# Sums of MLP weight blocks: from on-chip slots to a DRAM buffer, with plain loads into ten slots in turn

## The reference, cut to what matters

```
h = rms_norm(x);  z = h @ w_in                       # 1024 x 10240, split into ten parts
m = gated sum of three branches of z, each @ w_branch[i];  m = m @ w_out
x = x + rms_norm(m)
h = rms_norm(x)
f = square(relu(h @ w_ff1)) @ w_ff2                  # 1024 x 4096, 4096 x 1024
x = x + rms_norm(f)
```

## Time and profile before

| what | value |
|---|---|
| median of three runs | 962.34 us (958.67 to 963.13) |
| the profiled execution | 959.98 us, its span 958.2 us |
| PE busy | 948.2 us, 99% |
| DVE busy | 731.4 us, 76% |
| ACT busy | 430.6 us, 45% |
| POOL busy | 104.4 us, 11% |
| bytes moved | 142.84 MB, mean 149 GB/s |
| plain queue of SP (q1) | 111.32 MB, 32.7% of 16 engines' span |
| POOL's queue (q0), nearly all accumulating transfers | 27.27 MB, 15.4% |

### The profile page before, as it was taken

How to read it: one execution, slowest core, us unless ns; L and a number is a source line. 1 busy time by engine, 2 the same in 40 slices (tenths; PEclk the granted TensorE clock), 3 DMA queues, 4 the chain that set the end, 5 groups by cost and what they waited for, 6 DMA issues and landing times.

```text
span 958.2 us, 13425 instructions
## 1 busy us (share of the span) xinstructions
PE 948.2 (99%) x4838; PEld 809.0 (84%) x4838; DVE 731.4 (76%) x854; ACT 430.6 (45%) x534; POOL 104.4 (11%) x128
## 2 busy tenths in 40 slices
PE   9999999999999999999999999999999999999997
PEld 7888888888888888888888888899889889979985
DVE  4679888888888988886584434599976886796698
ACT  7632333333333322224274323467745745754674
POOL 1100001001100011113100000131101102011110
PEclk9999999999999999999999999999999999999998
DMA  8333223322222122223225333477989679678864
GB/s 325 110 111 105 99 93 96 108 93 93 93 95 102 66 100 96 89 89 132 88 93 215 109 109 110 176 198 192 269 265 245 162 212 246 172 185 260 246 188 132
DMA packets 40731, 142.84 MB, mean 149 GB/s; under 512 B 4720, under 2 KB 4848, under 8 KB 40688
## 3 DMA queue, kind: packets, MB, share of 16 engines
q1 hardware_dynamic: 31728, 111.32, 32.7%
q0 software_dynamic: 7712, 27.27, 15.4%
q10 hardware_dynamic: 1248, 3.67, 1.1%
HBM read 138.05 MB, written 4.19 MB: 148 GB/s over the span
## 4 chain that ended last, share of the span: by engine, by line
PE 82%; DMA 7%; DVE 6%; ACT 3%; issue 2%; SPq 0%; POOL 0%; DVEq 0%; ACTq 0%
PE ps L1590 25%; PE ps L1592 24%; PE ps L1594 24%; DMA glu<-units_in 5%; DVE w_lo L1066 3%; PE ps L1775 2%; PE ps L1779 2%; PE ps L1777 2%; DMA raw_d<-units_in 1%; ACT w_hi L683 1%; PE ps L1716 1%; DVE h_lo L1066 1%; PE ps L1670 1%; ACT h L960 1%; DVE h L1408 1%
## 5 line engine op out<-in xcount | busy, mean ns | idle before, releaser
L1590 PE MATMUL ps<-a_hi,w_hi 128*128 128x512 f32 x576 | 225.7, 392 | 0.0
L1066 DVE TENSOR_TENSOR w_lo<-raw,w_hi 128x1024 fp32r<-128x1024 f32 (+1 forms) x125 | 153.3, 1229 | 94.1 <-ACT w_hi L683 93.4
L1592 PE MATMUL ps<-a_lo,w_hi 128*128 128x512 f32 x576 | 224.2, 389 | 0.0
L1594 PE MATMUL ps<-a_hi,w_lo 128*128 128x512 f32 x576 | 224.1, 389 | 0.0
L683 ACT ACTIVATE w_hi<-raw 128x1024 fp32r<-128x1024 f32 (+1 forms) x125 | 130.2, 1048 | 186.1 <-PE ps L1594 112.9
L1149 DVE SCALAR_TENSOR_TENSOR conf<-glu,cols,conf (+1 forms) x240 | 186.8, 778 | 27.5 <-DVE conf L1149 26.4
L1590 PEld LDWEIGHTS ps<-a_hi,w_hi 128*128 128x128 f32 x576 | 108.1, 188 | 22.7 <-issue 0.5
L1592 PEld LDWEIGHTS ps<-a_lo,w_hi 128*128 128x128 f32 x576 | 108.1, 188 | 22.6 <-issue 0.5
L1594 PEld LDWEIGHTS ps<-a_hi,w_lo 128*128 128x128 f32 x576 | 108.2, 188 | 22.5
L1066 DVE TENSOR_TENSOR w_lo<-glu,w_hi 128x1024 fp32r<-128x1024 f32 x56 | 67.7, 1221 | 37.0 <-ACT w_hi L683 36.9
L1590 PE MATMUL ps<-w_hi,h_hi 128*128 128x512 f32 x224 | 87.9, 393 | 0.4
(11 more groups left out here) (177 smaller groups left out, 1608.7 us busy)
## 6 DMA issues: line engine op xcount, KB each, us to landing
raw<-units_in SPq DMA_DIRECT2D x141, 512.0 KB, 3.2
glu<-units_in SPq DMA_DIRECT2D x26, 512.0 KB, 6.5
glu<-units_in POOLq DMA_DIRECT2D x26, 512.0 KB, 8.3
raw_d<-units_in POOLq DMA_DIRECT2D x24, 512.0 KB, 6.5
raw_v<-units_in SPq DMA_DIRECT2D x16, 512.0 KB, 5.9
raw_d<-units_in SPq DMA_DIRECT2D x8, 512.0 KB, 6.2
conf<-x_in SPq DMA_DIRECT2D x4, 512.0 KB, 6.0
conf<-x_in ACTq DMA_DIRECT2D x1, 2048.0 KB, 8.0
```

The lines of the kernel that those rows point to most:

```text
L1066: return nc.vector.tensor_tensor(dst, src, hi, ALU.subtract)
L1590: nc.tensor.matmul(ps[:, bank, :], left_hi, right_hi, start=first, stop=False, skip_group_check=on_top)
L1592: nc.tensor.matmul(ps[:, bank, :], left_hi, right_lo, start=False, stop=False, skip_group_check=on_top)
L1594: return nc.tensor.matmul(ps[:, bank, :], left_lo, right_hi, start=False, stop=final, skip_group_check=on_top)
```

## The change

The sums of weight blocks are no longer made in the slots. A DRAM buffer `weight_sums` holds, for each of the eight matrices (four quarters, up and down), the four sums of two units each: 64 units of 512 KB.

- In each mixing tile ACT issues four copies of 1 MB, DRAM to DRAM, one for each sum of one matrix: its first block (`copy_first`). Before its third and later tiles it waits until the copies of two tiles before are done.
- POOL adds the second block of product 5's sum, one accumulating transfer of 1 MB per mixing tile, when that tile's copies are done, and the second block of product 7's sum, one per pair of the first gate stage (`two_blocks`). In the second gate stage it adds product 5's sum onto product 6's (`three_blocks`), in the third product 6's onto product 4's (`four_blocks`), one per pair, each behind a wait for the pair before. These transfers are written with a longest piece of 8192 bytes.
- In the MLP each unit is loaded by SP with one plain transfer of 512 KB, from the weights or from the sums, into slot (u - U_FF) mod 10, when the unit ten before it is split. SP waits for all sums ahead of the fifth load.
- `add_block`, `side_load`, `sum_beside`, `slot_of` and the waits that went with them are gone, on SP, POOL, ACT and DVE. PE's program is the same.

The core of the diff:

```
 # SP
-            def ff_load(q, f, product, halves=(0, 1)):
-                    if earlier_in_slot(u) and slot < RAW:
-                        sp.wait_ge(summed, sums_beside(q, f, h) - 2)
-                    elif earlier_in_slot(u):
-                        sp.wait_ge(w_lo_ready, earlier_in_slot(u)[-1] + 1)
+            def ff_load(u):
+                if u - U_FF >= SLOTS:
+                    sp.wait_ge(w_lo_ready, u - SLOTS + 1)
...
+                if product in PLAIN:
+                    src = units_d[U_FF + (2 * q + f) * BLOCK_UNITS + block_at(f, PLAIN[product]) + h]
+                else:
+                    src = sums_d[(2 * q + f) * BLOCK_UNITS + sum_at(product) + h]
+                sp.dma_start(slots[slot], src).then_inc(raw_loaded[slot], 16)
+            for n in range(4):
+                ff_load(U_FF + n)
+            for f in range(2):
+                sp.wait_ge(two_summed[f], 16 * QUARTERS)
+                sp.wait_ge(side_summed[f], 16 * QUARTERS)
+                sp.wait_ge(three_summed[f], 16 * QUARTERS)
+                sp.wait_ge(four_summed[f], 16 * QUARTERS)
...
 # POOL
+            def two_blocks(m, product, summed):
+                q, f = divmod(m, 2)
+                copies = len(SUMS) * (q + 1 if product == 5 else QUARTERS)
+                pool.wait_ge(first_copied[f], 16 * copies)
+                at = U_FF + m * BLOCK_UNITS + block_at(f, SECOND_BLOCK[product])
+                pool.dma_start(sum_of(m, product), units_d[at:at + 2].rearrange("h p n -> (h p) n"),
+                               accum_op=ALU.add, max_dma_last_dim=SUM_BYTES).then_inc(summed[f], 16)
+            def three_blocks(m):
+                f = m % 2
+                pool.wait_ge(two_summed[f], 16 * QUARTERS)
+                pool.dma_start(sum_of(m, 6), sum_of(m, 5), accum_op=ALU.add,
+                               max_dma_last_dim=SUM_BYTES).then_inc(three_summed[f], 16)
...
                 mask_spatial(j % 2, 32 * (j // 2 + 1))
+                if j:
+                    two_blocks(j - 1, 5, two_summed)
+            two_blocks(MATRICES - 1, 5, two_summed)
             for j in range(KT):
+                two_blocks(j, 7, side_summed)
                 pool.wait_ge(conf_tap, KT * (N_OWN + N_NEXT) + N_LATE * (j + 1))
...
+            for m in range(4, MATRICES):
+                behind_pair(KT + m)
+                three_blocks(m)
+            for m in range(MATRICES):
+                behind_pair(2 * KT + m)
+                four_blocks(m)
 # ACT
+            def copy_first(j, f, product):
+                source = j.times(BLOCK_UNITS, U_FF + block_at(f, FIRST_BLOCK[product]))
+                into = j.times(BLOCK_UNITS, sum_at(product))
+                act.dma_start(sums_d[bass.ds(into, 2)].rearrange("h p n -> (h p) n"),
+                              units_d[bass.ds(source, 2)].rearrange("h p n -> (h p) n")
+                              ).then_inc(first_copied[f], 16)
             def mix_tile(u, j, b):
+                if j.first >= 2:
+                    act.wait_ge(first_copied[b], Count(j.first // 2, j.i, 1).times(16 * len(SUMS)))
+                copy_first(j, b, 5)
                 after(u)
...
                 split_hi(u.plus(RING))
+                copy_first(j, b, 7)
...
                 split_hi(u.plus(3 + RING))
+                copy_first(j, b, 6)
...
                 split_hi(u.plus(4 + RING))
+                copy_first(j, b, 4)
```

More of the change, by code:

```diff
@@ L86 @@
 H_SLOT = {"22": 4, "22-21": 0, "11-21": 0, "11": 1, "21-22-11": 1, "12": 2, "21+12-11-22": 3}
-LOADED = {1: (0, 0), 2: (1, 0), 3: (1, 1), 5: (0, 0)}
-ADDED = {5: (0, 1), 6: (1, 1), 4: (1, 0), 7: (0, 1)}
+PLAIN = {1: (0, 0), 2: (1, 0), 3: (1, 1)}
+SUMS = (5, 7, 6, 4)
+FIRST_BLOCK = {5: (0, 0), 7: (1, 1), 6: (1, 1), 4: (1, 0)}
+SECOND_BLOCK = {5: (0, 1), 7: (0, 1)}
+SUM_ON_TOP = {6: 5, 4: 6}
+MATRICES = 2 * QUARTERS
 SLOTS = 10
-def slot_of(f, product):
-    return {1: 0, 2: 2, 3: 6, 7: 6}.get(product, 8 if f == DOWN else 4)
+SUM_BYTES = 8192
 def ff_unit(q, f, product, h):
@@ L105, in piece_of, with block_at, sum_at @@
     return q, f, ORDER[f][n // 2], n % 2
[L108 to L118, removed]
 def ff_slot(u):
[L122 to L127, removed]
+    return (u - U_FF) % SLOTS
 def ff_loads(u):
[L131 to L156, removed]
+    many = (u - U_FF) // SLOTS + 1
+    return 16 * (U_FF // RAW + many if ff_slot(u) < RAW else many)
+def block_at(f, block):
+    k_half, n_half = block
+    return 2 * (2 * k_half + n_half) if f == UP else CH * n_half + 2 * (1 - k_half)
+def sum_at(product):
+    return 2 * SUMS.index(product)
 def up_bank(q, product):
@@ L508, in side_load @@
[L508 to L516, removed]
+            def ff_load(u):
+                q, f, product, h = piece_of(u)
+                slot = ff_slot(u)
+                if u - U_FF >= SLOTS:
+                    sp.wait_ge(w_lo_ready, u - SLOTS + 1)
+                elif slot < 2:
+                    sp.wait_ge(w_lo_ready, u - RAW + 1)
+                elif slot < 4:
+                    sp.wait_ge(spatial_done, KT)
+                    sp.wait_ge(a_step, 3 * KT)
+                    sp.wait_ge(s_step, 3 * KT)
+                elif slot < 6:
+                    sp.wait_ge(y_c_lo, KT)
+                elif slot < 8:
+                    sp.wait_ge(mixed_in, 4 * CH)
+                else:
+                    sp.wait_ge(mixed_kept[CH - 2 + h], 16)
+                    sp.wait_ge(sumsq_ready, 4 * CH)
+                if product in PLAIN:
+                    src = units_d[U_FF + (2 * q + f) * BLOCK_UNITS + block_at(f, PLAIN[product]) + h]
+                else:
+                    src = sums_d[(2 * q + f) * BLOCK_UNITS + sum_at(product) + h]
+                sp.dma_start(slots[slot], src).then_inc(raw_loaded[slot], 16)
@@ L517, in _ @@
+            for n in range(4):
[5 more added lines that the diff above has]
+                sp.wait_ge(four_summed[f], 16 * QUARTERS)
+            for n in range(4, 6):
+                ff_load(U_FF + n)
             for c in range(CH):
                 if c == CH - 1:
-                    ff_load(0, UP, 3)
+                    for n in range(6, 8):
+                        ff_load(U_FF + n)
@@ L549, in _ @@
+            for u in range(U_FF + 8, UNITS):
+                ff_load(u)
             sp.wait_ge(unit_done, ff_unit(QUARTERS - 1, UP, 4, 1) + 1)
@@ L629, in _, with behind_pair @@
                                             ALU.add).then_inc(chan_sum, 1)
+            def behind_pair(n):
+                pool.wait_ge(unit_done, U_GATE + 2 * n)
+            for m in range(3):
+                behind_pair(KT + m)
+                three_blocks(m)
             for j in range(1, KT):
+                if j == KT // 2:
+                    behind_pair(KT + 3)
+                    three_blocks(3)
                 pool.wait_ge(squared, j + 1)
@@ L1469, in _ @@
                     split_behind(q, UP, 2, 1)
-                    for h in range(2):
-                        sum_beside(q, UP, h)
                 done(q, UP, 5, 0)
@@ L1539, in _ @@
                         add_product(q, product, 0)
-                    if product == 3 and q < QUARTERS - 1:
-                        sum_beside(q, DOWN, 1)
                     last_set = {1: "21+12-11-22", 2: "21-22-11", 3: "11-21"}.get(product)
@@ L1544, in _ @@
                         set_lo(q, last_set)
-                    if product == 2 and q < QUARTERS - 1:
-                        sum_beside(q, DOWN, 0)
                     if q == QUARTERS - 1 and product == 6:
```

102 lines of the change are left out of this document (17 added, 85 removed).

## The result

The changed kernel takes 973.74 us, the median of 4 runs (970.06 to 979.38); the kernel before, with a fourth run beside the three of the table, 962.09 (958.67 to 963.13). The ratio is 1.0141, with a 95% interval of 1.0108 to 1.0175: slower by 1.4%. I had forecast no change.

A forecast was written before the change was run, and what follows sets the result against it. PE was taken as the bound, busy 948.2 of 958.2 us. The MLP's -1.1 us and nothing else took the profiled 959.98 to 958.9, a median of 961.2; range 957.5 to 966, at 52%.

The forecast's parts named there:

- In the next two stages DVE is freer and the same holds: Second and third gate stages: loads beside accumulations bring no loss, as worked out for the first gate stage.
- The waits for pairs stand where PE has already passed them: POOL's new waits ahead of accumulating transfers in the gate stages: claimed to hold nothing back, no cost.
- I take 0: Mixing stage: loss from loads meeting copies and accumulations taken as 0; full meetings in all seven tiles would cost 0.5 us.
- bearing strength of 11.6 us: Mixing stage: a load near the tile's start can take 9.1 + 2.5 = 11.6 us before anything is lost for good.
- cover of 1.6 us: End of first gate stage: channel sum ends at 428.87, PE uses it at 430.50; further DVE lateness costs PE equally.
- Mostly they don't, since the accumulation is issued only when the last copy has landed, by when that load is largely through: Mixing tile starts: load, copy and accumulation seldom meet fully; a full meeting makes 11.9 us, 0.3 too much.
- The transfers of a tile: Mixing tile: six loads 7.6, four copies 14.8, one accumulation 6.5: 28.9 us, 23 to 37, in a 33.78 us tile.
- The first rival: Mixing tile starts: loads meeting accumulation and copy take 13.5 us in every tile; +11.7 us, 972.9, or 987; chance 33%.
- rivals of the first gate stage: First gate stage: a 7.8 us accumulation falls on each pair's soonest due load; +10.3 us, 971.5; chance 8%.
- late sums: Third rival, SP's wait before the fifth MLP load: accumulations of 10.5 us overrun 44 us of cover; +7, 969; chance 2%.
- I take 1.1 us; the ends are 0 and 3.1: MLP: gain from closing two PE gaps, 0.47 and 0.60 us, that start at accumulating transfers; ten other gaps stay.
- 17 us, of which PE sees nothing: MLP: removing 14 DVE sums of 1.23 us frees 17 us; PE gains nothing, DVE being busy 250.48 of 309 us.

The follow-up runs named there:

- experiments 2: Changed kernel without the eight accumulating transfers of the second gate stage, so some sums lack a part: 959.51 us, ratio 1.0015 to the kernel before.
- 8: Changed kernel with the second gate stage's eight accumulating transfers cut to 64 KB each, POOL's instructions and waits kept: 959.21 us, ratio 0.9988.
- experiment 3: Changed kernel with one sum in place of three behind the channel sum, one at the fourth square, the others two pairs later: 969.49 us, ratio 1.0095.
- experiment 5: Changed kernel with copies spread over the mixing tile and the second gate stage's sums moved later, into third gate stage and MLP: 954.96 us, ratio 0.9942.
- experiment 6: Sums as in experiment 5, but the copies placed as in the changed kernel: 959.69 us, ratio 0.9993.
- experiments 4: Changed kernel with a mixing tile's four copies one behind each of splits two to five, none at the tile's start; sums unchanged: 968.23 us, ratio 1.007.
- experiment 9: Changed kernel without copies and accumulating transfers, plain MLP blocks for sums, DVE's 14 sums put back as 28 half-tile passes: 957.9 us, ratio 0.9966.
- 1: Changed kernel with no copies and no accumulating transfers; the MLP loads a plain block in place of each sum: 955.34 us, ratio 0.9947.
- 10: As experiment 5, with copies and sums cut into pieces of 4096 bytes: 955.26 us, ratio 0.994.

## Why the prediction was wrong, point by point

- **The step that failed** is "In the next two stages DVE is freer and the same holds": a price of nothing for the sums of the second gate stage, carried over from the first without a row of the second. I looked at DVE's busy time there and not at the chain that runs through the stage: load, splits on ACT and DVE, squares on ACT, sums on POOL, PE's product at 464.04, which had 5.2 us of cover. What the runs showed in its place: loads that land in 3.2 us alone took 11.8 and 14.9 us, the chain was some 13 to 16 us late, and PE lost 7.7 us there and 3.7 at place 3. Without those eight sums, or with 64 KB in place of 1 MB, 1.3 to 1.5% comes back (1.0141 against 1.0015 and 0.9988, experiments 2 and 8).
- **With it failed** "The waits for pairs stand where PE has already passed them". I took a wait that holds nobody for one without a price. POOL comes late from the channel sum, finds the waits met and issues three at once, and two more behind the square sums. How much of the loss is that they go together stays open: with one in place of three (experiment 3) the ratio fell from 1.0141 to 1.0095, with overlapping intervals, and single sums made loads late as well.
- **"I take 0" in the mixing stage** was wrong too, and smaller. The bearing strength of 11.6 us came near in the sum alone: loads of 14.6, 14.0 and 11.75 us (the last issued at 227.87) exceed it by 3.0 + 2.4 + 0.15 = 5.6, and DVE was 4.63 late at the end; tile by tile it doesn't fit. The cover of 1.6 us held to a tenth. What I had wrong is how the transfers meet: "Mostly they don't, since the accumulation is issued only when the last copy has landed, by when that load is largely through". The load is issued behind the accumulation (87.20 after 86.46), and ACT issues the next two copies, 1.1 to 1.9 us apart, a few microseconds behind the load. Three tile starts of seven had a long wait. It cost 3.3 us in the profile of the changed kernel, and 4.7 between the medians of experiments 5 and 6.
- **The transfers of a tile** were well sized: 28.9 us forecast, 0.79 x 33.78 = 26.7 measured. A copy took 32.1% x 237.8 / 28 = 2.7 us of all engines (3.7 taken, 2.5 the lower end). The Trainium skill's page "DMA: Bandwidth & Descriptors", section "Latency and other measured facts", has 207 GB/s for copies between HBM tensors with rows 512 KiB apart and 214 with a padded pitch, which makes 5.0 us, an estimate; here a copy is one contiguous run of 1 MB, and the measurement, some 385 GB/s, decides. A sum in DRAM took, from 430 to 530, 51.1% of 100 us for 9.77 MB, or 5.5 us for 1.05 MB (6.5 taken, 5.3 the lower end). An average share below 1 said nothing about single loads, and I had given it too much weight.
- **The first rival** named a total of 972.9, near the measured one, by a collision in all seven tiles at 13.5 us. That mechanism was there, but worth 3.3 us, not 11.7; the agreement is chance. The rivals of the first gate stage and of late sums didn't come. In experiments 4 and 5, with the first gate stage's accumulations as in the change, PE is busy there throughout; in the changed kernel most loads of that stage landed in 3 to 7 us, as the prediction had worked out. The last sum landed at 597.3, and SP issued the fifth MLP load at 617.82, right behind the fourth (617.15). (The third rival's +7 makes 968, not 969.)
- **The MLP's gain**, "I take 1.1 us; the ends are 0 and 3.1", was mis-sized: 4.65. I had let ten of the 12 late starts stand; two small ones are left. And I had counted late starts above 0.12 us only and left out 25 between 0.02 and 0.12, which sum to 1.9. Further, "17 us, of which PE sees nothing" is refuted by experiment 9: a DVE that is busy 250 of 309 us was late for PE in places, for up to 2.7 us.

By ratios the parts add up: the MLP -0.5% (1), making the sums outside the second gate stage some +0.4 to 0.7% (2, 6 and 8 against 1), the sums inside it +1.3 to 1.5% (the change against 2, 6 and 8).

What stays open: that place 3 hangs on the two sums behind the square sums is read from traces; experiments 2, 6 and 8 took away all sums of that stage or their bytes, and none these two alone. That three going at once, and not three in that stage, makes most of place 2 rests on the trace and on experiment 3, whose gain is not clear of the noise. And the spread of the runs, 14 us in experiment 3, is explained in part at most: with the copies as in the change DVE came out of the mixing stage 4.0 to 7.0 us late in the profiles of the change and of experiments 2, 3, 6 and 8, and their runs spread over 6 to 14 us; those of 5 and 10 spread over less than 1.

## What to carry to other kernels

Work that is moved under another stage "because the engines are idle there" is to be charged load by load: ask which transfer with a deadline stands behind it, how late it may come, and which chain then waits, through every engine to the product that needs it. A mean share of the DMA engines of 0.8 in the mixing stage was harmless with the copies in one order (experiment 5) and cost 4.7 us in another (experiment 6). And a wait that is already satisfied is no pacing: where an engine arrives late, everything behind such waits goes out at once. Pacing alone is no cure either, while a single sum issued right ahead of a load can make it late.

## What the runs showed of the hardware

- PE idle for 4.4 us came back at the lower clock level, 0.50 granted for 6 us; after 2.0 us idle at 516.9 a dip to 0.53 followed as well. These two waits cost nearly twice their length (7.7 and 3.7 us). Behind the wait of 1.68 us in experiment 3 the granted clock stayed at 1.00 (615.5 to 618.5).
- A DRAM to DRAM copy of 1 MB took 2.7 us of the 16 engines, little more than plain loads of as many bytes (2.5 by the earlier trace rows); an accumulating transfer of 1 MB with source and destination in DRAM about 5.5, near the 5.3 of one to SBUF by the earlier trace rows.
- Pieces of 4096 bytes in place of 64 KB (copies) and 8 KB (sums), both shortened together, took 0.7% off the changed kernel by the ratios (1.0141 to 1.0072) at the same bytes, and nothing off the well ordered one (0.9942 and 0.994).
